# A two-block transformer kernel: six raw slabs with the rests written over them, another order of the buffers, the router's weights as the stationary operand

## The reference, cut to what matters

```
def moe_swiglu(h, router_w, w1, w3, w2):
    ...
    logits = jnp.einsum('td,de->te', t, router_w).astype(jnp.float32)
    top_vals, top_idx = lax.top_k(logits, TOP_K)
    top_w = jax.nn.softmax(top_vals, axis=-1)
    gates = jnp.sum(jax.nn.one_hot(top_idx, N_EXPERTS, dtype=jnp.float32) * top_w[..., None], axis=1)
    ...
    for e in range(N_EXPERTS):
        a = t @ w1[e]
        b = t @ w3[e]
        out = out + gates[:, e:e + 1] * ((jax.nn.silu(a) * b) @ w2[e])
...
        bias = rel_bias[t5_bucket(t_pos[None, :, None] - idx)]
```

## Time and profile before

| | |
|---|---|
| median of 3 runs | 3084.37 us (3081.85 to 3086.14) |
| profiled execution | 3082.72 us, span 3080.9 us |
| TensorE | busy 2892.0 us, 94% of the span |
| DVE, ACT | 67%, 55% |
| mean granted clock of TensorE | 0.966 |
| DMA | 633.63 MB, mean 206 GB/s |

### The profile page before, as it was taken

How to read it: one execution, slowest core, us unless ns; L and a number is a source line. 1 busy time by engine, 2 the same in 40 slices (tenths; PEclk the granted TensorE clock), 3 DMA queues, 4 the chain that set the end, 5 groups by cost and what they waited for, 6 DMA issues and landing times.

```text
span 3080.9 us, 34324 instructions
## 1 busy us (share of the span) xinstructions
PE 2892.0 (94%) x13334; PEld 2373.8 (77%) x13334; DVE 2063.1 (67%) x2910; ACT 1697.4 (55%) x2271; POOL 32.9 (1%) x55
## 2 busy tenths in 40 slices
PE   7998899999887999999999989989899999898998
PEld 6887688788765888888888868877778788776786
DVE  5576655556663898889888965478655454587553
ACT  5545254555532777777777754355454444555543
POOL 0000000000001000000000000000000000000000
PEclk9998899999987999999999989999999999999999
DMA  6443455454432999999999965544455555444453
GB/s 220 152 129 118 135 170 187 151 177 137 135 114 98 342 349 338 344 350 345 340 340 352 346 233 184 189 138 160 141 172 185 171 190 185 142 159 150 163 184 111
DMA packets 173657, 633.63 MB, mean 206 GB/s; under 512 B 19520, under 2 KB 19520, under 8 KB 173488
## 3 DMA queue, kind: packets, MB, share of 16 engines
q1 hardware_dynamic: 170752, 621.88, 59.1%
q0 software_dynamic: 2736, 9.49, 0.9%
HBM read 629.20 MB, written 2.10 MB: 205 GB/s over the span
## 4 chain that ended last, share of the span: by engine, by line
PE 85%; DVE 10%; ACT 3%; issue 1%; DMA 1%; SPq 0%; DVEq 0%; ACTq 0%; POOLq 0%
PE ps L1304 26%; PE ps L1306 25%; PE ps L1305 25%; DVE wlo L737 2%; PE ps L1416 2%; DVE CA L1180 2%; PE ps L1493 1%; PE ps L1540 1%; PE ps L1336 1%; PE ps L1403 0%; PE ps L1402 0%; DVE XN L905 0%; DVE Z L1267 0%; PE ps L1604 0%; DMA raw<-in_W 0%
## 5 line engine op out<-in xcount | busy, mean ns | idle before, releaser
L737 DVE TENSOR_TENSOR wlo<-raw,whi 128x1024 fp32r<-128x1024 f32 x1182 | 1395.4, 1222 | 553.0 <-ACT whi L301 542.4
L301 ACT ACTIVATE whi<-raw 128x1024 fp32r<-128x1024 f32 x1182 | 1199.4, 1058 | 600.5 <-PE ps L1306 542.7
L1304 PE MATMUL ps<-whi,XH 128*128 128x512 f32 (+1 forms) x2192 | 873.8, 399 | 42.6 <-DVE XL L755 17.7
L1305 PE MATMUL ps<-wlo,XH 128*128 128x512 f32 (+1 forms) x2192 | 859.1, 392 | 0.0
L1306 PE MATMUL ps<-whi,XL 128*128 128x512 f32 (+1 forms) x2192 | 859.1, 392 | 0.0
L1304 PEld LDWEIGHTS ps<-whi,XH 128*128 128x128 f32 x2192 | 418.9, 191 | 136.4 <-DVE XL L755 22.0
L1306 PEld LDWEIGHTS ps<-whi,XL 128*128 128x128 f32 x2192 | 418.0, 191 | 87.4
L1305 PEld LDWEIGHTS ps<-wlo,XH 128*128 128x128 f32 x2192 | 419.4, 191 | 82.7 <-issue 0.5
L1304 PE MATMUL ps<-whi,XEH 128*128 128x512 f32 x704 | 283.6, 403 | 1.4 <-DVE XEL L986 1.4
L1306 PE MATMUL ps<-whi,XEL 128*128 128x512 f32 x704 | 278.5, 396 | 0.0
L1305 PE MATMUL ps<-wlo,XEH 128*128 128x512 f32 x704 | 278.1, 395 | 0.0
(11 more groups left out here) (358 smaller groups left out, 2464.6 us busy)
## 6 DMA issues: line engine op xcount, KB each, us to landing
raw<-in_W SPq DMA_DIRECT2D x1182, 512.0 KB, 5.3
GP<-in_ffn_post_g POOLq DMA_DIRECT2D x4, 512.0 KB, 3.8
X<-in_x SPq DMA_DIRECT2D x1, 1024.0 KB, 5.0
skew<-RB POOLq DMA_DIRECT2D x4, 256.0 KB, 2.8
RB<-skew POOLq DMA_DIRECT2D x8, 128.0 KB, 2.4
GP<-in_mix_post_g POOLq DMA_DIRECT2D x2, 512.0 KB, 3.9
out<-X SPq DMA_DIRECT2D x1, 1024.0 KB, 4.0
mload<-in_cum_sums POOLq DMA_DIRECT2D x1, 768.0 KB, 8.7
```

Source lines behind the costliest of these rows:

```text
L301: act.activation(k.whi[:, slot, part], k.raw[:, slot, part], ACT.Copy).then_inc(*k.up("act_hi"))
L737: dve.tensor_tensor(k.wlo[:, slot, part], k.raw[:, slot, part], k.whi[:, slot, part], ALU.subtract).then_inc(*k.up("dve_lo"))
L1304: pe.matmul(ps, xh, k.whi[:, slot, cols], start=first, stop=False)
L1305: pe.matmul(ps, xh, k.wlo[:, slot, cols], start=False, stop=False)
```

## The change

- `raw` has six slabs and `wlo` is laid over it: DVE writes the rest of a slab where the slab lies (`place_of`). `whi` keeps three. SP loads slab n once slab n-6 has been multiplied, both halves at once.
- The order of the buffers is now raw/wlo, whi, XH, XL, region z, X, XN, region b, small ones and the router's tables (RW, RWS, iota, ltri), which leave region z.
- The router's weights, the iota and the triangular matrix are loaded or made at the start; DVE converts them after the first mixer (`router_tables`), and spreads the bias after the second layer's mixer (`bias_rows`).
- Logits: the split weights side by side (RWS, 128 x 16) are the stationary operand, 256 columns of XH or XL move: 16 matmuls, each pair of channels as soon as its XL is there. DVE copies the 16 x 256 result, TensorE turns it twice, DVE adds the two halves with the scale.
- DVE's order: copy, reciprocal, logits, both selections, SEL, exp's input, XN, positions, PM of the first expert, then the gates, the flag. `first_max` has one step fewer. TensorE no longer waits for the flag ahead of the gather.
- The distances and ACT's copy of them go into the first expert, behind its first up group (`distances`); its down matmuls wait for the copy.

```diff
     def memory(self):
-        self.raw = self.sb("raw", [P, RING, SLAB])
+        r = self.overlays("region_w", RAW * SLAB, [("raw", [P, RAW, SLAB], F32)], [("wlo", [P, RAW, SLAB], F32R)])
+        self.raw, self.wlo = r["raw"], r["wlo"]
         self.whi = self.sb("whi", [P, RING, SLAB], F32R)
-        self.wlo = self.sb("wlo", [P, RING, SLAB], F32R)
+        self.XH = self.sb("XH", [P, KT, S], F32R)
+        self.XL = self.sb("XL", [P, KT, S], F32R)
+        n = 9 * SEG
+        z = self.overlays("region_z", n, [("Z", [P, n], F32)], [
...
         self.X = self.sb("X", [P, NT, D])
         self.XN = self.sb("XN", [P, NT, D])
...
@@ Sync.slabs
-            slot = self.slot()
+            slot = self.place_of()
+            if self.n >= RAW:
+                sp.wait_ge(k.of("pe_slab"), self.n - RAW + 1)
             for h in range(2):
                 part = slice(h * HALF, (h + 1) * HALF)
-                if self.n >= RING:
-                    sp.wait_ge(k.of("dve_lo"), 2 * (self.n - RING) + h + 1)
                 sp.dma_start(k.raw[:, slot, part], k.a["W"][base + self.n, :, part]).then_inc(k.of(f"land{slot}{h}"), 16)
@@ Vector.lo
-                dve.tensor_tensor(k.wlo[:, slot, part], k.raw[:, slot, part], k.whi[:, slot, part], ALU.subtract).then_inc(*k.up("dve_lo"))
+                dve.tensor_tensor(k.wlo[:, at, part], k.raw[:, at, part], k.whi[:, slot, part], ALU.subtract).then_inc(*k.up("dve_lo"))
@@ Tensor, new
+    def distances(self, g):
+        pe, k = self.eng, self.k
+        if g:
+            return
...
+        pe.wait_ge(*k.at("rbb"))
+        pe.wait_ge(*k.at("hot"))
+        pe.wait_ge(*k.at("e.flag"))
+        for h in range(4):
+            mm = pe.matmul(k.ps[:, 4 + h, :], rbb[:, h, :], k.bias_tmp[0:REL_BUCKETS, 4:4 + 2 * S], start=True, stop=True)
+        mm.then_inc(*k.up("pe_prod", "dist"))
@@ Scalar, new
+    def distances(self, g):
+        act, k = self.eng, self.k
+        if g:
+            return
+        act.wait_ge(*k.at("dist"))
+        act.activation(k.RB[:].rearrange("p t h l -> p (t h l)").rearrange("p (h l) -> p h l", h=4), k.ps[:, 4:8, :], ACT.Copy).then_inc(*k.up("act_step", "distc"))
@@ Tensor.moe
-        for t in range(NT):
-            n = 0
-            for c in range(KT):
-                for xx, ww in ((k.XH, k.RWH), (k.XH, k.RWL), (k.XL, k.RWH), (k.XL, k.RWL)):
-                    mm = pe.matmul(ps[:, 6, t * NE:(t + 1) * NE], xx[:, c, t * P:(t + 1) * P], ww[:, c, :], start=n == 0, stop=n == 4 * KT - 1)
-                    n += 1
+        for c in range(KT):
+            if c % 2 == 0:
+                pe.wait_ge(*k.at(f"e.n{c // 2}.l"))
+            pe.matmul(ps[0:2 * NE, 6, 0:S], k.RWS[:, c, :], k.XH[:, c, :], start=c == 0, stop=False)
+            mm = pe.matmul(ps[0:2 * NE, 6, 0:S], k.RWS[:, c, :], k.XL[:, c, :], start=False, stop=c == KT - 1)
+        mm.then_inc(*k.up("pe_prod", "e.lt"))
+        pe.wait_ge(*k.at("e.ltc"))
+        for t in range(NT):
+            mm = pe.transpose(ps[:, 7, t * 2 * NE:(t + 1) * 2 * NE], k.LT[0:2 * NE, t * P:(t + 1) * P], k.ident[0:2 * NE, 0:2 * NE])
+        mm.then_inc(*k.up("pe_turn", "e.lg"))
@@ Vector.first_max
-        self.step(dve.tensor_tensor(A, src, bc(m), ALU.is_equal))
-        self.step(dve.tensor_tensor(A, A, RI, ALU.mult))
+        for t in range(NT):
+            x = dve.scalar_tensor_tensor(out=A[:, t, :], in0=src[:, t, :], scalar=m[:, t:t + 1], in1=RI, op0=ALU.is_equal, op1=ALU.mult)
+        self.step(x)
@@ Vector.moe
+        dve.wait_ge(*k.at("e.lt"))
+        dve.tensor_copy(k.LT[0:2 * NE, :], ps[0:2 * NE, 6, 0:S]).then_inc(*k.up("dve_step", "e.ltc"))
+        dve.wait_ge(*k.at("e.n.rms"))
+        self.step(dve.reciprocal(rs, rs), "e.n.rs")
         dve.wait_ge(*k.at("e.lg"))
+        for t in range(NT):
+            x = ts(B[:, t, :], ps[:, 7, t * 2 * NE:t * 2 * NE + NE], rs[:, t:t + 1], None, ALU.mult)
+        self.step(x)
+        for t in range(NT):
+            x = dve.scalar_tensor_tensor(out=LG[:, t, :], in0=ps[:, 7, t * 2 * NE + NE:(t + 1) * 2 * NE], scalar=rs[:, t:t + 1], in1=B[:, t, :],
+                                         op0=ALU.mult, op1=ALU.add)
+        self.step(x)
...
```

More of the change, by code:

```diff
@@ L40 @@
 RING = 3
+RAW = 6
 LEAD = 2
@@ L114, in memory @@
     def memory(self):
-        self.raw = self.sb("raw", [P, RING, SLAB])
+        r = self.overlays("region_w", RAW * SLAB, [("raw", [P, RAW, SLAB], F32)], [("wlo", [P, RAW, SLAB], F32R)])
+        self.raw, self.wlo = r["raw"], r["wlo"]
         self.whi = self.sb("whi", [P, RING, SLAB], F32R)
-        self.wlo = self.sb("wlo", [P, RING, SLAB], F32R)
+        self.XH = self.sb("XH", [P, KT, S], F32R)
+        self.XL = self.sb("XL", [P, KT, S], F32R)
+        n = 9 * SEG
+        z = self.overlays("region_z", n, [("Z", [P, n], F32)], [
+            ("GH", [P, FT, S], F32R), ("GL", [P, FT, S], F32R),
+            ("SG", [P, 3, NT, S], F32), ("GN", [P, 3, NT, S], F32),
+        ], [
+            ("GH_", [P, FT, P], F32R), ("GL_", [P, FT, P], F32R),
+            ("SG_", [P, 3, S], F32), ("GN_", [P, 3, S], F32),
+            ("XEH", [P, KT, P], F32R), ("XEL", [P, KT, P], F32R),
+            ("PM", [P, NT, P], F32),
+            ("PT", [P, S], F32R),
+            ("YH", [P, D], F32R), ("YL", [P, D], F32R),
+            ("GB", [P, D], F32), ("mo", [P, 512], F32), ("LT", [P, S], F32),
+        ], [
+            ("Z2", [P, 12 * NT * CW], F32),
+            ("HP", [P, 2, 30 + S], F32), ("CA", [P, 2, S], F32), ("CB", [P, 2, S], F32),
+            ("QT", [P, 2, S], F32), ("KTT", [P, 2, S], F32), ("QI", [P, 2, S], F32),
+            ("LG", [P, 4, S], F32), ("SCO", [P, 2, S], F32), ("WRK", [P, 2, S], F32), ("m8", [P, 16], F32),
+        ])
@@ new lines, in memory @@
+        self.Z, self.GH, self.GL, self.SG, self.GN, self.GH_, self.GL_ = (z[n] for n in ("Z", "GH", "GL", "SG", "GN", "GH_", "GL_"))
+        self.SG_, self.GN_, self.XEH, self.XEL, self.PM, self.PT, self.YH = (z[n] for n in ("SG_", "GN_", "XEH", "XEL", "PM", "PT", "YH"))
+        self.LT = z["LT"]
+        self.YL, self.GB, self.mo, self.Z2, self.HP, self.CA, self.CB, self.QT = (z[n] for n in ("YL", "GB", "mo", "Z2", "HP", "CA", "CB", "QT"))
+        self.KTT, self.QI, self.LG, self.SCO, self.WRK, self.m8 = (z[n] for n in ("KTT", "QI", "LG", "SCO", "WRK", "m8"))
@@ L171, in memory @@
[L171 to L174, removed]
@@ L299, in hi @@
                 part = slice(h * HALF, (h + 1) * HALF)
-                act.wait_ge(k.of(f"land{slot}{h}"), 16 * (self.n // RING + 1))
-                act.activation(k.whi[:, slot, part], k.raw[:, slot, part], ACT.Copy).then_inc(*k.up("act_hi"))
+                act.wait_ge(k.of(f"land{at}{h}"), 16 * (self.n // RAW + 1))
+                act.activation(k.whi[:, slot, part], k.raw[:, at, part], ACT.Copy).then_inc(*k.up("act_hi"))
             self.n += 1
@@ L1041, in moe @@
         x.then_inc(*k.up("dve_step", "e.xn"))
[L1042 to L1059, removed]
-        for t in range(NT):
[L1061 to L1067, removed]
+        dve.wait_ge(*k.at("e.cum"))
+        self.step(ts(A, ps[:, 5, 0:16].rearrange("p (t e) -> p t e", t=NT), 1.0, None, ALU.add))
+        self.step(tt(A, A, SEL, ALU.mult))
+        self.step(ts(POS, A, -1.0, None, ALU.add))
+        self.slots("x", 0, POS)
         dve.wait_ge(*k.at("e.w2e"))
@@ L1304, in slab @@
             pe.matmul(ps, xh, k.whi[:, slot, cols], start=first, stop=False)
-            pe.matmul(ps, xh, k.wlo[:, slot, cols], start=False, stop=False)
+            pe.matmul(ps, xh, k.wlo[:, at, cols], start=False, stop=False)
             mm = pe.matmul(ps, xl, k.whi[:, slot, cols], start=False, stop=last)
```

135 lines of the change are left out of this document (66 added, 69 removed).

## The result

| | before | after |
|---|---|---|
| median of the runs, us | 3084.12 (3081.85 to 3086.14) | 3031.47 (3029.06 to 3034.01) |
| profiled execution, us | 3082.7 | 3030.9 |
| its span, us | 3080.9 | 3029.1 |

What follows compares the result with a forecast made beforehand. The prediction took TensorE, busy for 94% of the span, as the bound; router -29.0, distances +3.6, stall and 2 MB +1.0, ring 0 and place -12.0 made -36.4 us, from 3082.7 to 3046.3, median 3048, range 3028 to 3064.

Steps and rivals of the forecast that it cites:

- The router (-29.0): From X complete to the first expert: shorter logits, selections and chain, first expert starting at 965.6; gain 29.0 us, bounds 26 to 31.
- logits ahead of 1/rms, SEL 3.4 us behind it: Signs in the router: logits there before 1/rms, and SEL some 3.4 us after it.
- The distances in the first expert (+3.6, and 1.0 for the stall and the 2 MB): First expert: eight matmuls cost 3.6 us; ACT's stall and Pool's 2 MB together 1.0, bounds 0 and 6.
- The ring (0): Weight ring: loads released earlier gain at most 8.4 us; taken as 0, since TensorE waits for no weights in the experts.
- The place of the operands (-12.0): Big matmuls: new buffer order brings experts' down matmuls (6.5 us) and GH's loads (5.5) from 233 to 227 ns.
- the bound of 6.2 ns x 4,488 = 27.8: Upper bound of the place term: all big pairs with GH and XEH at 227 ns, 27.8 us in all.
- both on one side of a line between 114,336 and 127,520 fits all four: Guess that a pair is quick when both operands lie on one side of an address line, taken at 114,560.
- The four pairs: Paces behind the line: whi with XH 227 ns, whi with XEH or GH 233, YH with PT 227, mcum with LFH 231.
- nor its alignment (PT's is that of XEH): Place argument: the stationary operand's alignment alone ruled out as cause, since PT shares XEH's alignment.
- The rival of no gain from place (3060): Place of operands gives nothing and only the router gains: -24.4 us, 3060; chance 0.23.
- The sum: Whole kernel: -29.0 + 3.6 + 1.0 - 12.0 = -36.4 us, giving a median of 3048.
- the first rival's 3032: All big pairs come to 227 ns: -29.0 + 4.6 - 27.8 = -52.2 us, 3032; chance 0.21.

Runs made afterwards that it cites:

- experiment 10: Changed kernel with the distances spread over TensorE's gaps in the router and LFH moved by 128 bytes: 3026.69 us.
- experiment 8: Changed kernel with the old ring of three and region z moved by 32 bytes: 3062.46 us.
- experiment 7: Kernel before with the change's ring of six alone: 3079.85 us, ratio 0.9985.
- experiment 1: Changed kernel with region z (GH, GL, XEH, XEL, PT, YH) moved by 32 bytes: 3057.47 us, ratio to before 0.9911.
- experiment 3: Changed kernel with only the rings (raw, wlo, whi) moved by 32 bytes: 3091.16 us, ratio to before 1.0024.
- experiment 9: Changed kernel with both tiles of a family at one distance from the rings: GH, GL 256; XEH, XEL 128; GH_, GL_ 4 bytes: 3047.37 us.
- experiment 5: Changed kernel with six distances from whi: GH 256, GL 128, GH_ 16, GL_ 4, XEH 64, XEL 192 bytes; XH, XL at 0: 3055.19 us.
- experiment 11: The changed kernel itself, unaltered, run again on the same chip as the candidate with spread distances: 3032.05 us.
- experiments 4 and 6: 4: changed kernel with the old ring of three, 3044.97 us; 6: changed kernel with rings, XH, XL and region z moved together by 32 bytes, 3034.35 us.

## Why the prediction was right and wrong

**The router (-29.0): right.** From X complete to the first expert 50.7 us fell to 21.8, 28.9 less. The steps fit too: logits ahead of 1/rms, SEL 3.4 us behind it, PM done 14.6 us after X is complete (I had 14.8).

**The distances in the first expert (+3.6, and 1.0 for the stall and the 2 MB): right with the ring of six.** The eight matmuls take 3.69 us at a granted clock of 1.00, and experiment 10 gets 3.9 back in this stage by taking them out; of the 1.0 us some 0.2 came. With six slabs the stall does just fit, and no wait of TensorE for wlo is left there. With three the first expert takes 3.3 us more (experiment 8).

**The ring (0): the number held for the kernel as it was, and not for the kernel as it became.** I argued from before that TensorE waited for no weights, and experiment 7 bears that out. But I had said myself that a quicker pace wants weights faster, and that ACT would stand behind the distances, and priced the old ring against neither: in the changed kernel it costs 5 us at the old pace and 10.5 to 13.5 at the new one. The change's parts depend on each other: by the medians the place is worth 3062.46 - 3044.97 = 17.5 us with three slabs and 26.0 with six, and by the traces the two are 4 us apart instead of 8.5 (experiment 8).

**The place of the operands (-12.0): the step that failed.** Direction and outline were right: pairs of operands have two paces by where they lie, and the bound of 6.2 ns x 4,488 = 27.8 is nearly what came, 26.0 by the medians. (The stages with these matmuls, five down projections and the eight experts, give 23.7 us between the traces of experiment 1 and the changed kernel, 5.3 ns a matmul.) What failed is "both on one side of a line between 114,336 and 127,520 fits all four", and with it the 12.0. No run shows the term or its line at 114,560, or a line anywhere: XEH and XEL, which by the line were to stay at 233 ns, went to 227, and in its place the runs showed a pace that goes with the distance of the two starts. The four pairs were fitted as well by a phase. I dismissed it with "nor its alignment (PT's is that of XEH)": that looked at the stationary tile alone, while YH, which moves past PT, has the same phase as PT, and whi has another than XEH. Asked of the pair, the rows of before had already said it: distances modulo 256 of 0 (whi and XH), 0 (YH and PT), 32 (whi and XEH or GH), 128 (mcum and LFH); quick, quick, slow, slow. (The prediction also has whi move to the middle; it lay in the middle of the rings before, and lies at their end now. Nothing was reckoned from that.)

What the runs measured, for this form (fp32r, 128 x 128 stationary, 512 columns moving, a new stationary tile for each matmul, granted clock 1.00): where the stationary and the moving tile start at the same place modulo 256 bytes, the mean step of XH, GH, GH_, XEH and their rests is 227 to 229 ns, and where they don't, 229 to 237. Seen quick are the distances 0 (XH in every run but experiment 3, 227 ns; GH in the changed kernel, 227.0) and 256 (GH in experiment 9, 227.0). Seen slow: 4, 16, 32, 64, 128, 192, 288, 320 and -32 (-32 is XH in experiment 3, 233.3 ns). Both steps around a stationary tile that is off are slow (232.5 and 234.0 ns around GL in experiment 5). The few steps with PT, at distance 0, hold to neither: 224 to 236 ns, and the earlier trace rows show quick ones.

The rival of no gain from place (3060) would have given no difference between the changed kernel and experiments 1 and 3. The runs with 32 bytes of padding measure 26 and 60 us: where the two operands start does matter in this kernel. Why it does is not shown.

**The sum.** Experiment 1 against before: -26.3 (my terms without place: -24.4; by the profiled executions it is -24.9, so most of the difference is the spread between executions). Place with six slabs: -26.0 (I had -12.0). Together -52.3, and 52.7 were measured. The difference to the forecast is 14.0 us of place and about 2 of that spread. The range held the result because it was drawn to reach both cases of place, not because the line was right. That the first rival's 3032 is met to within 1 us is luck in part: its 27.8 of place are about 2 too many, its 24.4 for the rest about 2 too few.

## What to carry to other kernels

Lay stationary and moving operands of large matmuls at the same start modulo 256 bytes (shown here for fp32r alone, 227 ns a step against 233), and test a suspicion of place by a pad of 32 bytes before looking for other causes; it costs a line or two and here moved 26 and 60 us. When the same matmul form has different steps from start to start with different tiles, compare what the *pair* has in common, not one side. And a buffer that is worth next to nothing in the kernel as it is (here 0 to 3 us for the ring, and 10.5 to 13.5 after the rest of the change) has to be priced again at the pace, and with the stalls, that the rest of the change makes: take the worth of a change's parts together, not one by one.

## What the hardware showed besides

- The slow step is 6.3 ns longer on average with GH and GL (227.0 to 233.3 ns over 1,300 steps, distance 0 and 288). Not every distance costs the same: with GH_ and GL_ at 4 bytes the three kinds of step take 231.2 to 233.3 ns, where they took 227.6 to 228.1 at 0; over all slow pairs the means lie between 229 and 237 ns.
- TensorE's granted clock differs between executions of the same kernel. From 15 to 30 us it was 1.00 in the profiled execution of the changed kernel and 0.66 in that of the same kernel in experiment 11, and from the first weight matmul to the first feed-forward's down projection it took 490.9 and 493.5 us. Busy time by stage, first the one, then the other:

```profile
15.00:30.00 15.00, 10.47 (x40) 8.57 (x41) 10.95 (x35) 13.51 (x22) 0.00 (x0) 1.00 0.82 314
```

```profile
15.00:30.00 15.00, 10.40 (x34) 8.36 (x35) 10.88 (x35) 13.60 (x22) 0.00 (x0) 0.66 0.77 276
```

  So 2 to 3 us between two profiled executions in their first stage mean nothing. Those of experiments 4 and 6 seem to be of this kind: the same stretch was granted 0.66 in both. Before the change it was 0.67, so some 2 us of the difference between the two main profiles are probably the clock's too.
- In experiment 10 TensorE's idle times in the router were at most 2.8 us (4.6 in experiment 11), with the 3.1 us of matmuls of heads 3, 0 and 1 put in between, and from 950 to 960 us it was still granted only half the clock (row below), as in experiment 11 (0.51).

```profile
950.00:960.00 10.00, 9.21 (x36) 7.68 (x37) 6.07 (x22) 2.74 (x4) 2.13 (x4) 0.51 0.14 53
```
